# A two-layer mixer with mixture of experts: a semaphore for each piece of expert weights, down weights released in halves, and expert sums in another order

## The chip, the cores and the metric

One core of a Trainium2 chip runs the whole program. Its engines work side by side and are tied together by semaphores: TensorE (PE) for products and transposes, VectorE (DVE), ScalarE (ACT), GpSimd (POOL), and SyncE (SP), which here does nothing but issue DMAs. Weights come from HBM by DMA. The metric is the device time of one execution in microseconds (us), the median over runs.

## What is computed

Two layers work on 256 latent and 256 context tokens of width 1024. Each has three token mixers, merged by gates, and then a mixture of 32 experts, of which each token takes two. Layer 0 sends all 512 tokens through its experts, layer 1 only the 256 latent ones. All is fp32. What the change touches is the second half of a layer:

```
def hierarchical_moe(h, ...):          # top-1 group, top-2 expert
    ...
    return expert_dispatch(h, experts, weights, w_gate, w_up, w_down)
def run_block(args):                   # one expert
    xb, e = args
    return (jax.nn.silu(xb @ w_gate[e]) * (xb @ w_up[e])) @ w_down[e]
...
x = x + mx[5] * fx                     # fx: weighted sum of a token's two experts
...
y = xf * lax.rsqrt(jnp.mean(xf * xf, axis=-1, keepdims=True) + NORM_EPS)   # next norm
```

## The kernel before

**Experts.** A layer's expert loop runs over 32 experts in pairs (`expert`, `s` is the expert's place in its pair). An expert has 64 slots of tokens; where the router sends it more (`n > BLK`), `more_slots` works through an extra block of 32 ahead of the 64. PE does, for each expert: `gate_up`, the product of its tokens with gate and up weights (line L795, 16 matmuls, which the profile shows as 32 records); then half of the preparation of the next pair (picking its token rows by a one-hot product, L779, or turning them, L787); `turn_h`; and `down`, the down product (L808, 8 matmuls, 16 records). ACT and DVE do the activation between the two and copy the result out, and ACT writes it to the HBM table `y_rows`.

**Weights.** An expert has four pieces of gate/up weights and two of down weights, 1 MB each, each two rows of the contraction: `gate_up` uses piece k // 2 in its step k. SP issues all pieces on one queue. Gate/up weights have two slots in the loop (a third, with id 2, serves only expert 1), down weights two. All four pieces of a slot raise one semaphore (`gu_in`), and PE waits for the sum of four ahead of `gate_up`; so with the two down pieces (`wd_in`). A slot is given back in pieces on the gate/up side (`gu_used` rises after each second step of `gate_up`, and `next_gate_up` on SP waits piece by piece), and as a whole on the down side (`down_done`, `next_down`). SP works through its list in order: four gate/up pieces of an expert, then its two down pieces, each with its wait.

**Sums and the next norm.** After the loop, POOL gathers the two expert rows of each token from `y_rows`, in tiles of 128 tokens: four tiles in layer 0, two in layer 1. Per tile, ACT scales the first row (L1239), DVE adds the second one, scaled (L1658), PE turns the sum (L919), DVE adds it to the stream (`add_tile`, L1652), ACT squares it (`square_tile`, L1232), and PE averages the squares over the width (`mean_tile`, L909) into PSUM bank 6 for all tiles. Then one root on ACT (L980), one reciprocal on DVE (L1315) and the norm's scaling (L1331; at the very end L1327) follow. ACT's order at the end of layer 0 is: scale 0, scale 1, square 0, scale 2, square 1, scale 3, square 2, two weight tiles of the next layer (`round_first`), square 3, root. DVE does its part of those weight tiles and the next layer's gains after the last addition.

Of the kernel before, what the change touches and what calls it, by code (L numbers as in the profile page):

```python
# [24 lines left out]
ACT = mybir.ActivationFunctionType  # L25
# [112 lines left out]
def hybrid_block(nc, t, out, counts=None):  # L138
# [4 lines left out]
    with ctx:  # L143
# [40 lines left out]
        eps = sb("eps", [P, 1])  # L184
        route_w = sb("route_w", [P, 2, 4])
# [6 lines left out]
        def part(base, kib, size, *dims, dt=F32):  # L192
# [68 lines left out]
        names = """ident_in mean_in consts_in rows_in_done vecs_in router_in swa_in wst0 wst1 wst2 wst3 wst4 wst5 mwt0 mwt1 mwt2 mwt3 mwt4 mwt5 cond_in bias0 bias1 bias2  # L261
            bias3 gu_in0 gu_in1 gu_in2 wd_in0 wd_in1 y_saved yo_saved yt_saved yg_got0 yg_got1 yg_got2 yg_got3 out_saved
# [7 lines left out]
            gu_used silu_done hid_done hidt_done hidt_copied down_done y_copied  # L270
# [6 lines left out]
        gu_in, wd_in = [g[f"gu_in{i}"] for i in range(3)], [g[f"wd_in{i}"] for i in range(2)]  # L277
# [103 lines left out]
        def _(sp):  # L381
# [35 lines left out]
            def load_gate_up(e_src, slot, pieces=range(4)):  # L417

                for i in pieces:
                    sp.dma_start(wgu[slot][i], e_src(t["w_exp_gate_up"])[:, 2 * i:2 * i + 2]).then_inc(gu_in[slot].sem, 16)  # L420

            def load_down(e_src, slot):

                for i in range(2):
                    sp.dma_start(wd[slot][i], e_src(t["w_exp_down"])[:, 2 * i:2 * i + 2]).then_inc(wd_in[slot].sem, 16)
# [21 lines left out]
            for l in range(DEPTH):  # L447
# [19 lines left out]
                def next_down(e, s):  # L467
                    sp.wait_ge(g["down_done"].sem, NE * l + e - 1)
                    load_down(lambda w: w[l, bass.ds(e, 1)].rearrange("a p k n -> (a p) k n"), s)
# [16 lines left out]
        def _(pe):  # L486
# [115 lines left out]
            for l in range(DEPTH):  # L602
# [202 lines left out]
                def down(bank, src, w, sem):  # L805
                    for k in range(4):
                        for j in range(2):
# [6 lines left out]
                def more_slots(more, slot, landed, s, two):  # L814
# [15 lines left out]
                    pe.wait_ge(gu_in[slot].sem, landed * 64)  # L830
                    for k in range(KC):
                        at = MORE * k
# [8 lines left out]
                    pe.wait_ge(wd_in[s].sem, (PAIRS * l + two + 1) * 32)  # L841
                    for k in range(4):
                        for j in range(4):
# [15 lines left out]
                def expert(e, two, s, slot, nth):  # L859
# [20 lines left out]
                    pe.wait_ge(gu_in[slot].sem, landed * 64)  # L880
                    gate_up(s, wgu[slot])
# [11 lines left out]
                    pe.wait_ge(wd_in[s].sem, (PAIRS * l + two + 1) * 32)  # L893
                    down(4, hid_t, wd[s], g["down_done"].sem)
# [9 lines left out]
                def mean_tile(tile):  # L904
                    if tile == 0:
                        claim(6)
                    pe.wait_ge(g["sq_done"].sem, g["sq_done"].at(*after, tile))
                    for c in range(KC):
                        mm = pe.matmul(pv_bank[:, tile * P:(tile + 1) * P], mean_w[:, :], sq_tile[tile % 2][:, c, :],  # L909
                                       start=(c == 0), stop=(c == KC - 1))  # L910
                    mm.then_inc(g["mean_done"].sem, g["mean_done"].tick(*after, tile))

                for tile in range(nt):
# [14 lines left out]
                free[6] = (g["rstd_sqrt"], after)  # L928
# [10 lines left out]
        def _(act):  # L939
# [22 lines left out]
            def squares(l, which):  # L962
                w = width(l) if which != "n1" else NTOK
                if which == "n1" and l == 0:
                    act.wait_ge(g["in_copied"].sem, g["in_copied"].at(KC - 2))
                    act.wait_ge(g["prep"].sem, g["prep"].at("xt", KC - 1))
                for c in range(KC):
# [7 lines left out]
                root(l, which, KC - 1)  # L975

            def root(l, which, last):
                w = width(l) if which != "n1" else NTOK
# [868 lines left out]
```

## Time and profile before

| | |
|---|---|
| runs | 2032.97, 2038.33, 2045.43 us; median 2038.33 |
| profiled execution | 2040.66 us (span on the page 2041.3), mean granted PE clock 0.954 |
| busy | PE 1796.3 us (88%), DVE 694.2 (34%), ACT 519.4 (25%), POOL 154.9 (8%) |
| expert loop of layer 0 | first product 625.8, end of last down product 1121.2 |
| expert loop of layer 1 | first product 1507.1, end of last down product 2003.3 |
| bytes moved | 550.71 MB, mean 270 GB/s over the span |

A row of a timeline gives start, duration, engine, source line, operation, output and input, and in brackets how long the engine was idle ahead of it and what ended that. "DMA" as the releaser is the landing of a transfer.
### The profile page before, as it was taken

The page shows a single profiled execution, that of the slowest core. Times are in us where ns is not written, and L with a number is a line of the kernel's source. Part 1 is how long each engine was busy: PE and PEld are TensorE (multiplying, and loading weights), DVE is VectorE, ACT ScalarE, POOL GpSimd, SP SyncE. Part 2 cuts the span into 40 slices and gives each one's busy share as a digit, 9 for nine tenths or more (in the row PEclk, how much of TensorE's full clock was granted, in tenths as well). Part 3 has the DMA queues.
Part 4 walks back from the last instruction along what each step waited for, and adds up shares of the span by engine and source line. Part 5 has one row for each costly group of instructions (what it writes and reads, how often), then busy time and mean ns, then how long its engine had stood idle before and what let it go on. Part 6 is the DMA issues. An engine that isn't in the chain of part 4 may idle for free.

```text
span 2041.3 us, 26468 instructions
## 1 busy us (share of the span) xinstructions
PE 1796.3 (88%) x9291; PEld 1022.3 (50%) x9292; DVE 694.2 (34%) x1451; ACT 519.4 (25%) x1053; POOL 154.9 (8%) x190
## 2 busy tenths in 40 slices
PE   6999899999968999899999599999858998988985
PEld 3756666678743343334433487779723333333323
DVE  4465255445452111111111665663531111111113
ACT  4344444432230011011110454551311111011011
POOL 0062031000000000000000224310000000000000
PEclk9999999999988999999999699999979999999997
DMA  8356565223266999998999243334496999999992
GB/s 311 129 184 212 202 220 185 102 69 102 73 262 240 379 422 421 421 397 349 420 421 400 91 136 90 113 94 141 157 399 231 409 403 421 421 421 421 420 421 83
DMA packets 96058, 550.71 MB, mean 270 GB/s; under 512 B 14162, under 2 KB 15650, under 8 KB 42724
## 3 DMA queue, kind: packets, MB, share of 16 engines
q1 hardware_dynamic: 83108, 526.89, 65.8%
q0 software_dynamic: 4224, 11.35, 1.9%
q10 hardware_dynamic: 8640, 11.28, 1.5%
q8 instruction: 59, 0.97, 0.2%
q14 instruction: 27, 0.22, 0.0%
HBM read 537.15 MB, written 12.32 MB: 269 GB/s over the span
## 4 chain that ended last, share of the span: by engine, by line
PE 64%; DMA 20%; DVE 7%; ACT 4%; issue 3%; SPq 0%; ACTq 0%; POOL 0%; POOLq 0%; DVEq 0%
DMA moe<-in_w_exp_gate_up_dram 18%; PE ps L795 17%; PE ps L507 8%; PE ps L509 8%; PE ps L508 8%; PE ps L808 6%; PE ps L779 3%; PE ps L729 2%; PE ps L656 2%; PE ps L685 2%; PE ps L667 2%; DMA moe<-in_w_mod_dram 1%; PE ps L835 1%; DVE w_lo L1297 1%; PE ps L565 1%
## 5 line engine op out<-in xcount | busy, mean ns | idle before, releaser
L795 PE MATMUL ps<-moe,ht 128*64 128x512 f32 x1984 | 466.8, 626 | 69.4 <-DMA moe<-in_w_exp_gate_up_dram 47.8
L795 PEld LDWEIGHTS ps<-moe,ht 128*64 128x64 f32 x1984 | 145.7, 144 | 383.3 <-issue 309.4
L1633 DVE TENSOR_TENSOR arena<-aux,ps 128x256 f32<-128x256 f32 x64 | 27.0, 422 | 702.7 <-ACT aux L1205 702.7
L507 PE MATMUL ps<-ht_hi,w_hi 128*128 128x512 f32 (+1 forms) x704 | 253.3, 360 | 3.0 <-ACT arena L1092 1.6
L509 PE MATMUL ps<-ht_hi,w_lo 128*128 128x512 f32 (+1 forms) x704 | 244.7, 348 | 0.0
L508 PE MATMUL ps<-ht_lo,w_hi 128*128 128x512 f32 (+1 forms) x704 | 244.5, 347 | 0.0
L808 PE MATMUL ps<-moe,arena 128*64 128x512 f32 x1024 | 233.8, 598 | 2.6
L1297 DVE TENSOR_TENSOR w_lo<-ws,w_hi 128x1024 fp32r<-128x1024 f32 (+1 forms) x122 | 150.2, 1235 | 223.3 <-ACT w_hi L997 223.3
L997 ACT ACTIVATE w_hi<-ws 128x1024 fp32r<-128x1024 f32 (+1 forms) x122 | 125.2, 1026 | 183.7 <-PE ps L509 146.7
L507 PEld LDWEIGHTS ps<-ht_hi,w_hi 128*128 128x128 f32 x704 | 134.2, 191 | 25.5 <-issue 9.7
L509 PEld LDWEIGHTS ps<-ht_hi,w_lo 128*128 128x128 f32 x704 | 134.2, 191 | 16.9
L508 PEld LDWEIGHTS ps<-ht_lo,w_hi 128*128 128x128 f32 x704 | 134.5, 191 | 15.3
L808 PEld LDWEIGHTS ps<-moe,arena 128*64 128x64 f32 x1024 | 67.8, 136 | 131.4 <-issue 120.9
L1209 ACT ACTIVATE arena<-ps 128x512 f32<-128x512 f32 x64 | 38.2, 597 | 373.4 <-PE ps L808 373.4
L1750 POOL DMA_INDIRECT arena<-y_rows,dest x8 | 7.8, 979 | 1480.5 <-ACTq L1224 1478.6
L1205 ACT ACTIVATE aux<-ps 128x256 f32<-128x256 f32 x64 | 24.6, 385 | 357.0 <-PE ps L795 357.0
L779 PE MATMUL ps<-hr_hi,pick 128*128 128x512 f32 x204 | 88.8, 435 | 9.4 <-DVE pick L1559 9.4
L779 PE MATMUL ps<-hr_lo,pick 128*128 128x512 f32 x204 | 82.4, 404 | 0.0
L1205 ACT ACT_TABLE_LOAD x32 | 41.1, 1283 | 138.0 <-issue 138.0
L779 PEld LDWEIGHTS ps<-hr_hi,pick 128*128 128x128 f32 x204 | 39.6, 194 | 42.0 <-issue 30.8
L1733 POOL DMA_DIRECT2D aux<-in_rpb_a_dram x64 | 39.7, 628 | 180.0 <-DVE stat L1408 127.5
L667 PEld LDWEIGHTS ps<-ident,moe 128*128 128x128 f32 x320 | 34.3, 141 | 33.6 <-issue 31.9
(253 smaller groups left out, 2186.6 us busy)
## 6 DMA issues: line engine op xcount, KB each, us to landing
moe<-in_w_exp_gate_up_dram SPq DMA_DIRECT2D x248, 1024.0 KB, 19.9
moe<-in_w_exp_down_dram SPq DMA_DIRECT2D x128, 1024.0 KB, 17.9
ws<-in_w_in_dram SPq DMA_DIRECT2D x92, 512.0 KB, 4.3
moe<-in_w_mod_dram SPq DMA_DIRECT2D x29, 1536.0 KB, 6.7
y_rows<-arena ACTq DMA_DIRECT2D x164, 64.0 KB, 5.6
ws<-in_w_branch_dram SPq DMA_DIRECT2D x16, 512.0 KB, 3.6
ws<-in_w_out_dram SPq DMA_DIRECT2D x16, 512.0 KB, 3.5
ws<-in_w_exp_gate_up_dram SPq DMA_DIRECT2D x6, 1024.0 KB, 19.0
```

Of the source, the lines that this page charges most:

```text
L507: pe.matmul(ps[:, bank, 0:cols], w[:, k, :], a_hi, start=(i == 0), stop=False)
L508: pe.matmul(ps[:, bank, 0:cols], w[:, k, :], a_lo, start=False, stop=False)
L509: mm = pe.matmul(ps[:, bank, 0:cols], w_lo[:, slot, k, :], a_hi, start=False, stop=(k == rows[-1]))
L656: mm = pe.matmul(score_bank[:, hh, 0:n], q_of(kind)[HD * hh:HD * hh + HD, pair, q0:q0 + P], kt_of(kind, 2 * pair + hh)[:, keys], start=Tru ...
L667: mm = pe.transpose(prob_bank[:, tile, hh * P:(hh + 1) * P], prob[h % 2][:, hh, tile * P:(tile + 1) * P], ident[:, :])
L685: mm = pe.matmul(pv_bank[HD * hh:HD * hh + HD, 0:SEQ], v_of(kind, 2 * pair + hh, tile + (4 - n)), prob_t[hh][:, tile, :], start=(tile == 0 ...
L779: mm = pe.matmul(ps[:, 7 * half, :], pick[:, tile, :], rows[:, tile, 512 * half:512 * half + 512], start=(tile == 0 and rows is hr_hi), st ...
L795: mm = pe.matmul(ps[BLK * j:BLK * j + BLK, 2, :].rearrange("p (g n) -> p g n", g=2), xg[:, k, BLK * s:BLK * s + BLK], w[k // 2][:, k % 2, ...
L808: mm = pe.matmul(ps[BLK * j:BLK * j + BLK, bank, :], src[:, k % 2, BLK * (k // 2):BLK * (k // 2) + BLK], w[k // 2][:, k % 2, 512 * j:512 * ...
L997: nc.scalar.activation(high_part(i)[:, 0:m], ws[:, slot, 0:m, :], ACT.Copy) \
L1205: nc.scalar.activation(act_g, ps[:, 2, 0:256], ACT.Silu).then_inc(g["silu_done"].sem, 1)
L1297: v.tensor_tensor(w_lo[:, ws_slots[item], 0:m], ws[:, ws_slots[item], 0:m, :], high_part(i)[:, 0:m].bitcast(F32), ALU.subtract).then_inc(g ...
```

## The change

Each piece has a semaphore of its own (`gu_in` 3 x 4, `wd_in` 2 x 2), and PE waits for a piece right ahead of the step that uses it first, in `gate_up`, `down` and `more_slots`. The down product raises `down_used` after each of its two halves, and SP loads the halves of a down slot one by one. At the end of a layer ACT takes the order scale, scale, scale, square; averages alternate between banks 6 and 7; root and reciprocal are done for each tile; the next layer's first weight tiles and gains go ahead of the sums; and an activation with a one-column result (`load_roots`) loads ACT's table for roots ahead of the sums and ahead of the second norm.

```
-                sp.dma_start(wgu[slot][i], ...).then_inc(gu_in[slot].sem, 16)
+                sp.dma_start(wgu[slot][i], ...).then_inc(gu_in[slot][i].sem, 16)
...
                 def next_down(e, s):
-                    sp.wait_ge(g["down_done"].sem, NE * l + e - 1)
-                    load_down(lambda w: ..., s)
+                    for i in range(2):
+                        sp.wait_ge(g["down_used"].sem, 2 * (NE * l + e - 2) + i + 1)
+                        load_down(lambda w: ..., s, (i,))
...
-                def gate_up(s, w):
+                def gate_up(s, slot, landed):
+                    w = wgu[slot]
                     for k in range(KC):
+                        if k % 2 == 0:
+                            pe.wait_ge(gu_in[slot][k // 2].sem, landed * 16)
...
-                    mm.then_inc(sem, 1)
+                            if k % 2 and j:
+                                mm.then_inc(g["down_used"].sem, 1)
...
-                    pe.wait_ge(gu_in[slot].sem, landed * 64)
-                    gate_up(s, wgu[slot])
+                    gate_up(s, slot, landed)
...
                 def mean_tile(tile):
-                    if tile == 0:
-                        claim(6)
+                    claim(6 + tile % 2)
...
-                    if tile:
-                        mean_tile(tile - 1)
+                    if tile >= 2:
+                        mean_tile(tile - 2)
                 for bank in (2, 3, 4, 5):
                     claim(bank)
-                mean_tile(nt - 1)
+                for tile in range(nt - 2, nt):
+                    mean_tile(tile)
...
+            def load_roots():
+                nc.scalar.activation(root_one[:, :], eps[:, :], ACT.Sqrt)
...
+                load_roots()
+                if l + 1 < DEPTH:
+                    round_first(l + 1)
                 for tile in range(nt):
                     nc.scalar.activation(hr[:, tile, :], yg[tile][0], ACT.Copy, ...)
-                    if tile:
-                        square_tile(tile - 1)
-                if l + 1 < DEPTH:
-                    round_first(l + 1)
-                square_tile(nt - 1)
-                root(*after, nt - 1)
+                    if tile >= 2:
+                        square_tile(tile - 2)
+                for tile in range(nt - 2, nt):
+                    square_tile(tile)
+                    if nt > 2:
+                        root_tile(tile - 2)
+                for tile in range(nt - 2, nt):
+                    root_tile(tile)
```

The first place is PE's gate/up product of the first expert of a pair, in the loop over pairs. `moe_51` holds the weights, `ht_49` the tokens, `gu_in1` is the semaphore of slot 1. Before:

```order
L864 UNCONDITIONAL_BRANCH
L880 REGISTER_ALU
L795 MATMUL ps<-moe_51,ht_49 64x512 [waits gu_in1]
L795 MATMUL ps<-moe_51,ht_49 64x512 x15
L883 REGISTER_ALU
```

The same place afterwards (`gu_in10` to `gu_in13` are the four pieces of slot 1):

```order
L876 UNCONDITIONAL_BRANCH
L799 REGISTER_ALU
L801 MATMUL ps<-moe_51,ht_49 64x512 [waits gu_in10]
L801 MATMUL ps<-moe_51,ht_49 64x512 x3
L801 MATMUL ps<-moe_51,ht_49 64x512 [waits gu_in11]
L801 MATMUL ps<-moe_51,ht_49 64x512 x3
L801 MATMUL ps<-moe_51,ht_49 64x512 [waits gu_in12]
L801 MATMUL ps<-moe_51,ht_49 64x512 x3
L801 MATMUL ps<-moe_51,ht_49 64x512 [waits gu_in13]
L801 MATMUL ps<-moe_51,ht_49 64x512 x3
```

The single wait ahead of 16 matmuls is now four, one ahead of each four; no other instruction was added between them.

The second place is ACT at the end of layer 0. `route_w` marks the scalings, `arena<-xt` the squares, `aux<-ps,eps` the roots. Before:

```order
L1239 ACTIVATE arena<-arena,route_w 128x1024 [waits yg_got1]
L1232 ACTIVATE arena<-xt 128x1024 [waits comb_added]
L1239 ACTIVATE arena<-moe,route_w 128x1024 [waits yg_got2]
L1232 ACTIVATE arena<-xt 128x1024 [waits comb_added]
L1239 ACTIVATE arena<-moe,route_w 128x1024 [waits yg_got3]
L1232 ACTIVATE arena<-xt 128x1024 [waits mean_done,comb_added]
L997 ACTIVATE w_first<-ws 128x1024 [waits out_done,wst5]
L997 ACTIVATE w_hi<-ws 128x1024 [waits out_done,wst0]
L1232 ACTIVATE arena<-xt 128x1024 [waits mean_done,comb_added]
L980 ACT_TABLE_LOAD
L980 ACTIVATE aux<-ps,eps 128x512 [waits mean_done]
```

Afterwards:

```order
L1013 ACTIVATE w_first<-ws 128x1024 [waits out_done,wst5]
L1013 ACTIVATE w_hi<-ws 128x1024 [waits out_done,wst0]
L1261 ACTIVATE arena<-arena,route_w 128x1024 [waits yg_got0,dest_set]
L1261 ACTIVATE arena<-arena,route_w 128x1024 [waits yg_got1]
L1261 ACTIVATE arena<-moe,route_w 128x1024 [waits yg_got2]
L1251 ACTIVATE arena<-xt 128x1024 [waits comb_added]
L1261 ACTIVATE arena<-moe,route_w 128x1024 [waits yg_got3]
L1251 ACTIVATE arena<-xt 128x1024 [waits comb_added]
L1251 ACTIVATE arena<-xt 128x1024 [waits mean_done,comb_added]
L992 ACTIVATE aux<-ps,eps 128x128 [waits mean_done]
L1251 ACTIVATE arena<-xt 128x1024 [waits mean_done,comb_added]
L992 ACTIVATE aux<-ps,eps 128x128 [waits mean_done] x3
```

The third scaling went ahead of the first square and the fourth ahead of the second, the two weight tiles ahead of all scalings, and one root of 512 columns became four of 128.

The third place is PE at the end of layer 1, with two tiles. `hr` lies in `arena`; `mean_w` marks the averages. Before:

```order
L919 MATMUL ps<-ident,arena 128x128 [waits comb]
L919 MATMUL ps<-ident,arena 128x128 x7
L909 MATMUL ps<-arena,mean_w 128x128 [waits sq_done]
L909 MATMUL ps<-arena,mean_w 128x128 x7
L909 MATMUL ps<-arena,mean_w 128x128 [waits comb_added,sq_done]
```

Afterwards:

```order
L929 MATMUL ps<-ident,arena 128x128 [waits comb]
L929 MATMUL ps<-ident,arena 128x128 x7
L918 MATMUL ps<-arena,mean_w 128x128 [waits comb_added,sq_done]
L918 MATMUL ps<-arena,mean_w 128x128 x7
L918 MATMUL ps<-arena,mean_w 128x128 [waits sq_done]
```

The wait for the second tile's addition (`comb_added`) moved from the second average to the first.

## Rows read from the trace of the kernel before

**Rows 1.** The page, chain of work that ended last: shares of the span by line.

```profile
DMA moe<-in_w_exp_gate_up_dram 18%; PE ps L795 17%; PE ps L507 8%; PE ps L509 8%; PE ps L508 8%; PE ps L808 6%; PE ps L779 3%; PE ps L729 2%; PE ps L656 2%; PE ps L685 2%; PE ps L667 2%; DMA moe<-in_w_mod_dram 1%; PE ps L835 1%; DVE w_lo L1297 1%; PE ps L565 1%
```

**Rows 2.** Stretches: start:end, length, busy time by engine, PE clock, DMA share, GB/s.

```profile
692.00:752.00 60.00, 59.13 (x278) 23.62 (x274) 9.74 (x18) 7.80 (x12) 0.00 (x0) 1.00 1.01 410
896.00:972.00 76.00, 71.91 (x423) 30.17 (x417) 12.22 (x24) 8.82 (x14) 0.00 (x0) 0.98 0.90 356
972.00:1113.00 141.00, 134.25 (x620) 54.18 (x618) 24.34 (x45) 16.23 (x25) 0.00 (x0) 0.99 1.01 421
1637.00:1655.00 18.00, 17.57 (x85) 6.36 (x82) 2.47 (x5) 2.31 (x4) 0.00 (x0) 1.00 0.99 367
1836.37:1851.64 15.27, 12.20 (x60) 4.32 (x60) 2.47 (x5) 1.01 (x3) 0.00 (x0) 1.00 1.01 421
```

**Rows 3.** Timeline of PE, 1840 to 1910: two gate/up products of layer 1.

```profile
1851.63 8.78 PE L795 MATMUL ps<-moe,ht 128*64 128x512 f32 x32 [2.63 <-DMA moe<-in_w_exp_gate_up_dram]
...
1866.90 7.09 PE L795 MATMUL ps<-moe,ht 128*64 128x512 f32 x32 [0.59 <-DMA moe<-in_w_exp_gate_up_dram]
```

**Rows 4.** Timeline of SP's DMA issues, 840 to 1110: weights of expert 22.

```profile
954.28 5.48 SPq L420 DMA_DIRECT2D moe<-in_w_exp_gate_up_dram  x4
967.13 0.85 SPq L425 DMA_DIRECT2D moe<-in_w_exp_down_dram  x2
```

**Rows 5.** Timeline of PE, 836 to 960: expert 16 and expert 17's extra block.

```profile
865.68 8.78 PE L795 MATMUL ps<-moe,ht 128*64 128x512 f32 x32 [2.94 <-DMA moe<-in_w_exp_gate_up_dram]
...
888.68 5.35 PE L835 MATMUL ps<-moe,arena 128*32 128x256 f32 x64 [0.60 <-DVE arena L1617]
```

**Rows 6.** Timeline of PE, 1060 to 1125: experts 28, 30 and 31 of layer 0.

```profile
1062.75 8.78 PE L795 MATMUL ps<-moe,ht 128*64 128x512 f32 x32 [2.45 <-DMA moe<-in_w_exp_gate_up_dram]
...
1093.28 7.09 PE L795 MATMUL ps<-moe,ht 128*64 128x512 f32 x32 [1.64 <-DMA moe<-in_w_exp_gate_up_dram]
...
1108.56 7.09 PE L795 MATMUL ps<-moe,ht 128*64 128x512 f32 x32 [0.50 <-DMA moe<-in_w_exp_gate_up_dram]
...
1117.54 3.65 PE L808 MATMUL ps<-moe,arena 128*64 128x512 f32 x16
```

**Rows 7.** Timeline of PE, 1983 to 2005: last expert of layer 1.

```profile
1989.04 8.70 PE L795 MATMUL ps<-moe,ht 128*64 128x512 f32 x32 [2.29 <-DMA moe<-in_w_exp_gate_up_dram]
```

**Rows 8.** Timeline of PE's weight loads, 1100 to 1106: start of a down product.

```profile
1104.40 0.20 PEld L808 LDWEIGHTS ps<-moe,arena 128*64 128x64 f32 x4 [0.35 <-issue]
1104.89 0.14 PEld L808 LDWEIGHTS ps<-moe,arena 128*64 128x64 f32 x2 [0.28 <-issue]
```

**Rows 9.** Timeline of DVE, 1126 to 1166: sums, additions, next norm.

```profile
1137.72 2.15 DVE L1652 SCALAR_TENSOR_TENSOR xt<-ps,modv,xt 128x128 f32<-128x128 f32 x8
1142.04 1.28 DVE L1658 SCALAR_TENSOR_TENSOR arena<-moe,route_w,arena 128x1024 f32<-128x1024 f32 x1 [2.16 <-ACT arena L1239]
...
1148.76 4.22 DVE L1652 SCALAR_TENSOR_TENSOR xt<-ps,modv,xt 128x128 f32<-128x128 f32 x16
...
1161.67 2.46 DVE L1331 SCALAR_TENSOR_TENSOR ht<-xt,gain,aux 128x256 f32<-128x256 f32 x6
```

**Rows 10.** Timeline of ACT, 1126 to 1166: first scaling, a weight tile, table load, root.

```profile
1132.12 1.15 ACT L1239 ACTIVATE arena<-arena,route_w 128x1024 f32<-128x1024 f32 x1 [10.22 <-DMA arena<-y_rows,dest]
...
1151.91 1.04 ACT L997 ACTIVATE w_first<-ws 128x1024 fp32r<-128x1024 f32 x1
...
1154.86 1.28 ACT L980 ACT_TABLE_LOAD   x1
1157.56 0.69 ACT L980 ACTIVATE aux<-ps,eps 128x512 f32<-128x512 f32 x1 [1.42 <-PE ps L909]
```

**Rows 11.** Timeline of all engines, 1983 to 2042: averages and reciprocal at the end.

```profile
2022.64 5.64 PE L909 MATMUL ps<-arena,mean_w 128*128 128x128 f32 x32 [1.19 <-ACT arena L1232]
...
2028.90 1.75 DVE L1315 RECIPROCAL aux<-aux 128x256 f32<-128x256 f32 x1 [5.25 <-ACT aux L980]
```

**Rows 12.** The page, DMA issues: queue, KB each, median us from issue to landing.

```profile
moe<-in_w_exp_gate_up_dram SPq DMA_DIRECT2D x248, 1024.0 KB, 19.9
```

More of the change, by code:

```diff
@@ L419, in load_gate_up, with load_down @@
                 for i in pieces:
[L420 to L425, printed above, removed]
+                    sp.dma_start(wgu[slot][i], e_src(t["w_exp_gate_up"])[:, 2 * i:2 * i + 2]).then_inc(gu_in[slot][i].sem, 16)
+            def load_down(e_src, slot, pieces=range(2)):
+                for i in pieces:
+                    sp.dma_start(wd[slot][i], e_src(t["w_exp_down"])[:, 2 * i:2 * i + 2]).then_inc(wd_in[slot][i].sem, 16)
             held = []
@@ L803, in turn_h, with down @@
                     mm.then_inc(g["hidt_done"].sem, 1)
-                def down(bank, src, w, sem):
+                def down(bank, src, s, landed):
+                    w = wd[s]
                     for k in range(4):
+                        if k % 2 == 0:
+                            pe.wait_ge(wd_in[s][k // 2].sem, landed * 16)
                         for j in range(2):
@@ L892, in expert @@
                     pe.wait_ge(g["y_copied"].sem, done + 1)
[L893 to L894 removed]
+                    down(4, hid_t, s, PAIRS * l + two + 1)
                 for e in range(2 * AHEAD_PAIRS):
@@ L974, in squares, with root @@
                         .then_inc(g["sq_done"].sem, g["sq_done"].tick(l, which, c))
[L975 to L978 removed]
+                root(l, which, KC - 1, slice(0, w))
+            def root(l, which, last, cols, *tile):
                 act.wait_ge(g["mean_done"].sem, g["mean_done"].at(l, which, last))
[L980 to L981 removed]
+                bank = 6 + tile[0] % 2 if tile else 6
+                nc.scalar.activation(rs[:, cols], ps[:, bank, cols], ACT.Sqrt, bias=eps[:, 0:1]) \
+                    .then_inc(g["rstd_sqrt"].sem, g["rstd_sqrt"].tick(l, which, *tile))
+            def load_roots():
+                nc.scalar.activation(root_one[:, :], eps[:, :], ACT.Sqrt)
             def round_weights(l, job, ahead=2):
@@ L1226, in _, with root_tile @@
                 after = (l + 1, "n1") if l + 1 < DEPTH else (l, "fin")
+                def root_tile(tile):
+                    root(*after, tile, slice(tile * P, (tile + 1) * P), tile)
                 def square_tile(tile):
@@ L1316, in reciprocal_rms, with reciprocal_tile @@
                 dve.wait_ge(g["rstd_done"].sem, g["rstd_done"].at(l, which))
+            def reciprocal_tile(l, which, tile):
+                cols = slice(tile * P, (tile + 1) * P)
+                dve.wait_ge(g["rstd_sqrt"].sem, g["rstd_sqrt"].at(l, which, tile))
+                v.reciprocal(rs[:, cols], rs[:, cols]).then_inc(g["rstd_done"].sem, g["rstd_done"].tick(l, which, tile))
+                if tile == (4 if which == "n1" else 2) - 1:
+                    dve.wait_ge(g["rstd_done"].sem, g["rstd_done"].at(l, which, tile))
             def leave_h(l, c):
@@ L1350, in _ @@
                 w_all = width(l)
-                gains(l, 0)
-                if l:
-                    gains(l, 1)
-                    leave_first(l)
-                    reciprocal_rms(l, "n1")
+                if l == 0:
+                    gains(l, 0)
+                else:
+                    for tile in range(4):
+                        reciprocal_tile(l, "n1", tile)
                 scale_norm(l, "n1")
@@ L1663, in _ @@
                 dve.wait_ge(g["comb_added"].sem, g["comb_added"].at(l, nt - 1))
-            reciprocal_rms(DEPTH - 1, "fin")
+            for tile in range(2):
+                reciprocal_tile(DEPTH - 1, "fin", tile)
             scale_norm(DEPTH - 1, "fin")
```

32 lines of the change are left out of this document (20 added, 12 removed).

## The prediction

> **What bounds the kernel now.** I read the chain of work that ended last first [rows 1]: most of it is TensorE (PE), but its largest single entry is no instruction. It is the landing of gate/up weights, 18% of the span, some 367 us. Since that share is an average over two expert loops, I went on with the view of stretches [rows 2]. Its GB/s column reads 421 wherever DMA is never idle: from 972 to 1113 (end of the first loop) and in a single expert of the second one (15.27 us, of which PE is busy 12.20 at a granted clock of 1.00, its full level of 2.4 GHz). There DMA sets the pace, and no order of waits moves it: 6.29 MB of weights an expert at 421 GB/s is 14.9 us, the rest is rows of y. So the change can pay only where DMA was idle (692 to 752: 410; 896 to 972: 356; 1637 to 1655: 367), and after the last piece has landed, when PE alone is late.
>
> What PE does in a bound expert is in [rows 3]: 2.63 us without work, then 32 matmul records in 8.78; in the next one 0.59, then 7.09. The longer idle time costs 1.69 more, because the product begins at the lower clock. In both cases all four pieces had to be there, while at 421 GB/s a piece (1.05 MB) takes 2.49 us and its quarter of the product 7.09/4 = 1.77. PE could have been through three quarters when the fourth landed.
>
> **The change part by part.** *Products piece by piece.* Three places count.
>
> (a) Expert 16 of layer 0, just ahead of one whose extra block of 32 slots keeps PE longer. Its product starts at 865.68 after 2.94 idle and takes 8.78 [rows 5]. Afterwards one quarter is left when the last piece lands: 8.78 - 1.77 = 7.0 earlier. From there to about 1060 PE hardly waits, so the whole chain moves by 7.0. Expert 17's extra product (888.68 now) would start at 881.7; its last gate/up piece lands, two down pieces and four of its own behind the one at 865.65, at 865.65 + 6 x 2.49 = 880.6. That margin of 1.1 us is thin.
>
> (b) Then PE runs on until DMA stops it. Before, it waited 2.45, 1.64 and 0.50 in experts 28, 30 and 31 and lost 1.69 to the clock: 6.3 [rows 6]. If DMA moves ahead with PE, these go. DMA does: its issues at 954.28 and 967.13 wait for PE's releases [rows 4] and come 7.0 earlier, the second another half down product earlier (3.65/2 = 1.8). So DMA gets back 8.8 of the 11.7 it loses between 896 and 972 (76 x (1 - 356/421)). Two ends compete. PE's: 1121.2 (1117.54 + 3.65) less 7.0, 6.3 and the 1.5 of the next paragraph. DMA's: the last piece at 1108.5 - 8.8 - 1.5 = 1098.2, then 1.77, the 1.9 from product to down product, and 3.65: 1105.5. PE's is 1106.4, later, and decides.
>
> (c) The last expert of layer 1: its product, 8.70 after 2.29 idle [rows 7], becomes one quarter: 6.9. The down pieces land 2.5 and 5 us behind the last gate/up piece; the down product's halves want them 3.7 and 5.5 behind it. They are there.
>
> *Down weights released in two.* The first half is free 1.8 earlier. That matters once per stretch, where DMA runs dry on exactly this release: in layer 0, 60 x (1 - 410/421) = 1.6 us is lost between 692 and 752, of which I take 1.5 (ends 0 and 1.8); in layer 1, 18 x (1 - 367/421) = 2.3, part of it paced by PE's gate/up releases, which don't move: 1.0 (ends 0 and 2.3).
>
> *More waits.* Each product has four semaphores to look at instead of one, each down product two. PE's rows get no longer by it, the waits ride on matmuls. Weight loads that ran ahead may stop at them. The nearest row is the first load of a down product, which waits for several semaphores that are already up: 0.35 idle against 0.28 between loads [rows 8], so 0.07. On PE's path in layer 0 stand 15 experts x 4 waits: between 0 and 4.2; since the loads overlap running matmuls I take 1.0.
>
> So layer 0's loop: 7.0 + 6.3 + 1.5 - 1.0 = 13.8 (low end 6.8, which is the last product's 7.09 - 1.77 = 5.3 and 1.5; high end 16). Layer 1's: 6.9 + 1.0 = 7.9 (5.3 to 9.2).
>
> A rule speaks against waiting in small bits. First the rows: 0.59 idle left the clock up, 2.63 brought half of it for 8 of 32 records [rows 3]. The Trainium skill (TensorE: Matmul & The Clock Gate, section "A second HAM failure mode: psum-queue depth-cycling") says that frequent short idles between groups of matmuls make the clock swing between its levels even where no single one is long. In bound experts the change makes such idles, 2.49 - 1.77 = 0.7 after each piece. By the rows the sum stays as it is; by the rule it is the third rival's. No row here shows idles of 0.7 in a series.
>
> *Expert sums, end of layer 0.* Before, ACT scales tile 2 only after squaring tile 0, and tile 3 after squaring tile 1, so sums (1.28) and additions (2.15) on DVE have pauses between them: the first addition ends at 1139.87, the last at 1152.98 [rows 9], 13.1 for 2 sums and 3 additions, which are 9.0 of work. Afterwards the sums don't wait for squares, and this work can run back to back: 4.1 earlier, last addition at 1148.9. It wants tile 3 on DVE at 1143.3, so gathered by about 1142. From the last addition to the norm's first product it was 8.7 (to 1161.67), with a root of 0.69 for 512 columns in it [rows 10]. Afterwards both last averages follow the last addition, since they stand behind the claim of all transpose banks: 5.64 for two [rows 11]; then a root of 128 columns, at most 0.69, I take 0.4, and a reciprocal of 128, 0.95, a little over half of the 1.75 for 256 [rows 11]; with 0.3 of hops 7.3, so 1.4 less. That is 5.5, and the clock may be up for the averages: I take 6.0 (3.3 if gathers or a low clock hold the middle, 7.5 if neither). The gains and the first two weight tiles, moved ahead, lie in the 10.22 in which ACT waits for the first gather [rows 10], at no cost; without that cover ACT's half of them alone would be 2 x 1.04. The table of roots, 1.28, moves there too; where it was, it ran beside the averages and cost nothing.
>
> *Second norm.* The same table load leaves the place between last square and root, where the last average runs beside it: between 0 and 1.28 in each layer, I take 0.3, in sum 0.6. Its new place is ahead of ACT's wait for the first output product.
>
> *End of layer 1.* Only two tiles, so no round is saved. The first average now waits for the second tile's addition: 1.0 later than 2022.64. The reciprocal per tile gives back 0.8 (1.75 to 0.95), the root perhaps 0.1 [rows 11]. Sum -0.1 (-1.0 to 1.0).
>
> **Sum.** 13.8 + 7.9 + 6.0 + 0.6 - 0.1 = 28.2. Against the profiled execution's 2040.66 that is 2012.5. The median of the runs shown lies 2.3 lower, which would give 2010.1; I predict **2010**. The runs of this kernel spread from 2032.97 to 2045.43, so a change under 1% (20 us) can hardly be told from none.
>
> **The rivals.** *The gap of layer 0 stays.* Expert 17's pieces are late, or the issues stay bunched: PE's 7.0 is eaten at the thin margin of (a), DMA comes no earlier, and the loop gains its low end, 6.8. Sum 21.2, time 2017. For it: 1.1 us of margin. Against: the releases come from PE, which is earlier by itself. Chance 0.13.
>
> *It doesn't do what it says.* The four pieces are in flight together and share the 16 DMA engines; landing takes 19.9 us from issue [rows 12], in which several pieces could advance side by side and land together. Then PE still waits for the last one with all its work to do; (a), (b) and (c) go, and 1.5 + 1.0 + 6.5 = 9 remains: 2029. For it: nothing shows single landings. Against: they are issued 1.8 apart on one queue, the 19.9 fits eight pieces in line at 2.49. Chance 0.08.
>
> *The clock swings at the short waits.* Last quarter, the way to the down product and the down product (1.77 + 1.9 + 3.65 = 7.3) then run at half speed, 7.3 more, which takes (a) and (c) and most of (b): 28.2 - 7.0 - 6.9 - 5 = 9, about 2029. Against: 0.59 idle did no harm. Chance 0.06.
>
> *Slower than before.* Where PE stays at the lower clock through the DMA-bound stretches, an expert's 12.20 becomes 24.4, 9.1 more than DMA's 15.27. Eighteen experts of layer 1 are bound so; from four in a row on (28.2/9.1 = 3.1) the gain is gone, with six it is 2067 - some 26 above before. For it: the rule above. Against: a PE that is late has no idle time, and in the row of 8.78 the clock was back within one product. Chance 0.04.
>
> **How the numbers follow.** The forecast has 0.69, between 2002 (16 + 9.2 + 7.5 + 1.9 + 1.0 = 35.6 off, 3 below by the runs' spread) and 2018. To hold 8 in 10, the range must reach over the first rival and its spread: 2002 to 2023. Faster by over 1% means under 2018: most of the forecast and half the first rival, 0.73; slower 0.04; the rest 0.23.
>
> **What would show it.** Waits of products for weights become many short ones of under 1 us each, and the last product of a loop has pauses within it. Stretch rows of the first loop: 356 becomes 400 or more. Wrong by: products that still wait 2 to 3 us and then run through (second rival), PE clock below 0.9 in bound experts of both parities (third), a first-loop end less than 10 us earlier with the pauses there (first).

## The result

The changed kernel takes 2014.61 us, median of four runs (2012.05 to 2019.42), against 2038.51 before (2032.97 to 2045.43). The ratio is 0.9885, 95% interval 0.9868 to 0.9901: 1.15% or 23.4 us faster, where 28.2 were forecast against the profiled execution and 2010 as the time. A second set of runs gave 0.9869 (0.9853 to 0.9886). Below, a loss against the changed kernel in us is the difference to the mean of these two ratios, 0.9877, times 2039; the intervals leave some 4 to 5 us of doubt in each.

The two profiled executions lie 28.6 apart (2040.66 and 2012.05), their spans 31.0. That is 7 more than the medians (23.9), so the table below holds some 7 us of the spread between executions, and a term of it that matches the forecast within a few us says little by itself. In the seven profiles of this study that have both expert loops as changed, word for word, layer 0's loop takes 480.4 to 482.2 and layer 1's 482.3 to 488.4. By places, from the timelines of the two:

| from, to | before | after | change | forecast |
|---|---|---|---|---|
| start to first product of layer 0's expert loop | 625.8 | 624.3 | -1.5 | -0.3 |
| layer 0's loop, to the end of its last down product | 495.4 | 480.4 | -15.0 | -13.8 |
| to the first scaling of the next norm | 40.5 | 35.8 | -4.7 | -6.0 |
| to the first product of layer 1's loop | 345.4 | 344.5 | -0.9 | -0.3 |
| layer 1's loop | 496.2 | 486.0 | -10.2 | -7.9 |
| to the output's DMA | 33.6 | 34.8 | +1.2 | +0.1 |

(The last column takes the terms of the prediction, the 0.6 of the second norm halved between the layers.)

**The profile after.** The page's chain of work that ended last; in [rows 1] the weights' landing had 18%:

```profile
PE ps L801 15%; DMA moe<-in_w_exp_gate_up_dram 12%; PE ps L817 8%; PE ps L510 8%; PE ps L512 8%; PE ps L511 8%; PE ps L782 4%; SPq L422 2%; PE ps L732 2%; PE ps L659 2%; PE ps L688 2%; PE ps L670 2%; PE ps L568 1%; DVE w_lo L1321 1%; SPq L427 1%
```

The stretches of the changed kernel that answer to [rows 2] (start:end, length, busy time by engine, PE clock, DMA share, GB/s):

```profile
692.00:752.00 60.00, 59.13 (x276) 25.26 (x272) 10.57 (x20) 7.99 (x12) 0.00 (x0) 1.00 1.02 421
...
896.00:972.00 76.00, 71.89 (x403) 29.74 (x401) 13.76 (x27) 9.03 (x14) 0.00 (x0) 0.98 0.98 397
972.00:1113.00 141.00, 129.63 (x606) 52.78 (x602) 24.80 (x50) 18.65 (x29) 1.33 (x2) 0.99 0.99 408
...
1700.00:1960.00 260.00, 225.35 (x998) 74.36 (x992) 38.92 (x76) 28.22 (x43) 0.00 (x0) 1.00 1.01 421
```

410 became 421 and 356 became 397; the 408 of the third row comes from the loop, whose weights now end within it. The last row is the bound part of layer 1: DMA is as saturated as before, so its pace is unchanged, 15.28 an expert (16 of them from 1711.43 to 1955.94, by the starts of their products), and the PE clock there is 1.00.

The timeline of PE, changed kernel: the expert ahead of the extra block in layer 0 ([rows 5]), the last expert of layer 0 ([rows 6]) and the last one of layer 1 ([rows 7]):

```profile
854.09 1.94 PE L801 MATMUL ps<-moe,ht 128*64 128x512 f32 x8 [0.41 <-DMA moe<-in_w_exp_gate_up_dram]
856.58 1.94 PE L801 MATMUL ps<-moe,ht 128*64 128x512 f32 x8 [0.55 <-DMA moe<-in_w_exp_gate_up_dram]
859.28 1.94 PE L801 MATMUL ps<-moe,ht 128*64 128x512 f32 x8 [0.76 <-DMA moe<-in_w_exp_gate_up_dram]
862.22 1.94 PE L801 MATMUL ps<-moe,ht 128*64 128x512 f32 x8 [1.01 <-DMA moe<-in_w_exp_gate_up_dram]
...
878.27 5.16 PE L846 MATMUL ps<-moe,arena 128*32 128x256 f32 x64 [0.52 <-DVE arena L1648]
...
1090.98 5.32 PE L801 MATMUL ps<-moe,ht 128*64 128x512 f32 x24
1097.18 1.94 PE L801 MATMUL ps<-moe,ht 128*64 128x512 f32 x8 [0.88 <-DMA moe<-in_w_exp_gate_up_dram]
1101.02 3.65 PE L817 MATMUL ps<-moe,arena 128*64 128x512 f32 x16
...
1958.26 1.94 PE L801 MATMUL ps<-moe,ht 128*64 128x512 f32 x8 [0.44 <-DMA moe<-in_w_exp_gate_up_dram]
1960.75 1.94 PE L801 MATMUL ps<-moe,ht 128*64 128x512 f32 x8 [0.55 <-DMA moe<-in_w_exp_gate_up_dram]
1963.54 1.94 PE L801 MATMUL ps<-moe,ht 128*64 128x512 f32 x8 [0.85 <-DMA moe<-in_w_exp_gate_up_dram]
```

One wait of up to 2.9 us ahead of 32 records has become waits of 0.4 to 1.0 ahead of eight, four of them in the first product shown and three in the last. PE doesn't wait less: from 1690 to the end of layer 1 PE's waits for gate/up weights sum to 33.6 us in 20 waits before and 32.6 in 51 after, the longest 2.6 and 0.9. Where DMA sets the pace, a wait that is cut in pieces is still a wait. What pays is what PE has left when the last piece lands: 1.94 instead of 8.7.

### The profile page after: what moved, and what is told of

It reads as the page before. It is cut to its first block, busy times and chain, and to the rows that moved or that the text cites. A ratio compares the mean times of both kernels' runs of the same rounds, so it can differ in the third digit from the quotient of the medians.

```text
span 2010.3 us, 26521 instructions
## 1 busy us (share of the span) xinstructions
PE 1779.2 (89%) x9291; PEld 1010.1 (50%) x9292; DVE 693.2 (34%) x1455; ACT 520.9 (26%) x1061; POOL 155.6 (8%) x190
## 4 chain that ended last, share of the span: by engine, by line
PE 67%; DMA 13%; DVE 8%; ACT 4%; SPq 4%; issue 4%; POOL 0%; ACTq 0%; POOLq 0%; DVEq 0%
PE ps L801 15%; DMA moe<-in_w_exp_gate_up_dram 12%; PE ps L817 8%; PE ps L510 8%; PE ps L512 8%; PE ps L511 8%; PE ps L782 4%; SPq L422 2%; PE ps L732 2%; PE ps L659 2%; PE ps L688 2%; PE ps L670 2%; PE ps L568 1%; DVE w_lo L1321 1%; SPq L427 1%
## 5 line engine op out<-in xcount | busy, mean ns | idle before, releaser
L801 PE MATMUL ps<-moe,ht 128*64 128x512 f32 x1984 | 456.3, 603 | 59.7 <-DMA moe<-in_w_exp_gate_up_dram 39.4
L801 PEld LDWEIGHTS ps<-moe,ht 128*64 128x64 f32 x1984 | 136.5, 138 | 369.4 <-issue 259.6
## 6 DMA issues: line engine op xcount, KB each, us to landing
moe<-in_w_exp_gate_up_dram SPq DMA_DIRECT2D x248, 1024.0 KB, 20.3
```

What stands on the lines that cost most here:

```text
L801: mm = pe.matmul(ps[BLK * j:BLK * j + BLK, 2, :].rearrange("p (g n) -> p g n", g=2), xg[:, k, BLK * s:BLK * s + BLK], w[k // 2][:, k % 2, ...
```

## The experiments

**All four pieces awaited, the rest as changed.**

```
 for k in range(KC):
-    if k % 2 == 0:
-        pe.wait_ge(gu_in[slot][k // 2].sem, landed * 16)
+# ahead of the loop, in gate_up and more_slots:
+for i in range(4):
+    pe.wait_ge(gu_in[slot][i].sem, landed * 16)
```

> The changed kernel, but each gate/up product waits for all four of its pieces before its first step; down weights released in halves and the sums as changed. Theory (the piecewise wait carries most of the gain): expert 16's product and those of experts 28, 30 and 31 of layer 0 wait 2 to 3 us again and run through in 7.1 to 8.8, the loop of layer 0 ends 12 to 14 us later, the last product of layer 1 takes its whole 8.7 behind the last piece, 6.8 later; 2014.6 + 19 to 21 = 2034 to 2036. Rival (the four pieces land nearly together, the gain is from the halves and the sums): under 3 us later, 2015 to 2018.

Measured: 2032.74, ratio 0.9971 (0.9954 to 0.9988), 19 us above the changed kernel. The theory holds, the second rival of the prediction (pieces that land together) falls. The timeline of PE (experts 16 and 30 of layer 0, 29 and 31 of layer 1):

```profile
862.54 7.09 PE L801 MATMUL ps<-moe,ht 128*64 128x512 f32 x32 [2.95 <-DMA moe<-in_w_exp_gate_up_dram]
...
1087.70 7.09 PE L801 MATMUL ps<-moe,ht 128*64 128x512 f32 x32 [2.65 <-DMA moe<-in_w_exp_gate_up_dram]
...
1945.18 8.78 PE L801 MATMUL ps<-moe,ht 128*64 128x512 f32 x32 [2.27 <-DMA moe<-in_w_exp_gate_up_dram]
...
1975.71 7.09 PE L801 MATMUL ps<-moe,ht 128*64 128x512 f32 x32 [2.30 <-DMA moe<-in_w_exp_gate_up_dram]
```

Layer 0's loop is 491.2 long, 10.8 more than in the changed kernel and less than the 12 to 14 expected: the product of expert 16 ran in 7.09 after 2.95 idle, where before the change it took 8.78 after 2.94 [rows 5]. Of experts 28, 30 and 31 only 30 waited over 2 us; 28 and 31 waited 1.54 and 0.82. The clock's 1.69 thus isn't owed to the wait alone. The last two rows say the same: 2.27 and 2.30 idle, 8.78 and 7.09. The kernel before had shown it too: beside the rows of [rows 3] it has, in layer 1's expert 30, 7.09 after 2.62:

```profile
1973.77 7.09 PE L795 MATMUL ps<-moe,ht 128*64 128x512 f32 x32 [2.62 <-DMA moe<-in_w_exp_gate_up_dram]
```

Two stretches of the run that awaits all four, the first one in layer 0 and the second in layer 1 (the changed kernel has 397 GB/s and a clock of 1.00 there):

```profile
896.00:972.00 76.00, 71.27 (x403) 30.62 (x401) 14.06 (x28) 8.82 (x14) 0.00 (x0) 0.98 0.91 369
...
1700.00:1960.00 260.00, 227.14 (x986) 88.34 (x986) 39.27 (x77) 26.81 (x42) 0.00 (x0) 0.95 1.01 421
```

**Piecewise in layer 0 only.** In layer 1 all four are awaited, by the same edit under `if l`.

> The changed kernel, but only layer 0 waits piece by piece; in layer 1 each product waits for all four. Theory: layer 0's loop as in the changed kernel (480 from its first product to the end of the last down product); in layer 1 the last piece lands as early as in the changed kernel (478.6 after the loop's first product), since DMA sets the pace, and only the last product is late by 6.8; 2021.4. Rival (the piecewise waits also give pieces back earlier, and that brought DMA's 3.4 us in layer 1): the last piece lands at 481 to 482, 2023 to 2025.

Measured: 2024.23, ratio 0.9928 (0.9905 to 0.9950), 10.4 above the changed kernel, 9 below the one that waits for all four. Both layers have their share. The last product of layer 1, in the timeline of PE:

```profile
1965.74 7.09 PE L803 MATMUL ps<-moe,ht 128*64 128x512 f32 x32 [0.72 <-DMA moe<-in_w_exp_gate_up_dram]
```

It begins 480.5 after the loop's first product, between the 478.6 of the theory and the rival's 481. This can't be read closer: in the seven profiles that have both loops as changed, the last quarter begins 474.9 to 480.9 after it.

**Down halves released together.**

```
 for i in range(2):
-    sp.wait_ge(g["down_used"].sem, 2 * (NE * l + e - 2) + i + 1)
+    sp.wait_ge(g["down_used"].sem, 2 * (NE * l + e - 2) + 2)
```

> The changed kernel, but both halves of a down slot are loaded only when the whole down product is over. Theory (the early half feeds DMA where it runs dry): GB/s below 421 in the first 130 us of both loops, the last piece of layer 1 lands 3.4 later after the loop's first product (482 instead of 478.6), layer 0 ends 1 to 2 later; 2014.6 + 4.4 to 5.4 = 2019 to 2020. Rival (layer 0 is paced by PE from expert 18 on and has room, and DMA's 3.4 in layer 1 come from PE's earlier gate/up releases): under 1 us, 2014 to 2016.

Measured: 2023.25, ratio 0.9918 (0.9899 to 0.9937), 8.4 above the changed kernel: more than the theory asked. The stretches of layer 0:

```profile
621.00:692.00 71.00, 59.24 (x256) 23.02 (x258) 13.72 (x36) 6.49 (x10) 0.00 (x0) 0.93 0.73 275
692.00:752.00 60.00, 59.14 (x277) 23.95 (x274) 9.90 (x19) 8.16 (x12) 0.00 (x0) 1.00 1.01 416
...
896.00:972.00 76.00, 71.46 (x403) 30.02 (x401) 14.94 (x29) 8.83 (x14) 0.00 (x0) 0.98 0.95 386
```

DMA loses in three stretches, not in one: the changed kernel has 421 and 397 in the second and third (above; 421 to 422 and 395 to 403 in the seven profiles), and in the first 66.5 us from the loop's first product it has 303 GB/s (299 to 305), this run 293. Layer 0's loop is 4.3 longer than the changed kernel's and 2.5 longer than the longest of the seven. Expert 3's product took 8.8 instead of 7.1 here, by the clock; but it took 8.5 to 8.8 in three of the seven as well, whose loops are only 0.7 to 0.9 longer than the changed kernel's, so most of the 4.3 isn't the clock's.

**The halves alone, on the kernel before.** The down product raises its semaphore after each half and SP loads half by half; nothing else.

> The kernel before with one part of the change alone: the down product raises its semaphore after each half, and SP loads the halves of a down slot one by one. Theory, from the runs so far (the early half pays in every stretch in which DMA runs dry, three in layer 0 and two in layer 1): first loop 4.1 shorter (491.3 from its first product), second one 3.3 to 3.5 shorter; 2038.5 - 7.5 = 2031. Rival, the sum of the prediction (it pays once in each layer, 1.5 and 1.0): 2036.

Measured: 2036.22, ratio 0.9984 (0.9970 to 0.9998), 3.3 us below before. The interval leaves 0.4 to 6.1, so the theory of 7.5 falls; the rival, my own sum of 2.5, lies within it. In the profile the two loops are 0.6 and 1.3 shorter than before. In the stretches:

```profile
692.00:752.00 60.00, 59.13 (x276) 24.03 (x273) 10.16 (x19) 8.16 (x12) 0.00 (x0) 1.00 1.01 418
...
896.00:972.00 76.00, 71.90 (x401) 29.89 (x399) 12.22 (x24) 8.82 (x14) 0.00 (x0) 0.98 0.91 358
```

The third stretch keeps its hole (356 before, 358): its issues follow PE, and PE is as late there as before. The halves give 3.3 (0.4 to 6.1) without piecewise waits and 8.4 (some 4 to 13) with them. These intervals overlap, so the medians don't show that the parts depend on each other. The profiles speak for it: layer 0's loop gains 0.6 without the piecewise waits and 2.5 or more with them. That PE's earlier steps let the half release act between 896 and 972 fits the 358 and 397. At the loop's start it can't be the piecewise gate/up waits: the run that awaits all four has 299 GB/s over the first 66.5 us, this one 294. The two differ there in the down product, which waits piece by piece only in the former; no run undoes that wait alone, so this part stays open.

**The expert loops alone, end of a layer as before.** All of the change in the loops; scalings, squares, averages, roots, reciprocals, gains and first weight tiles in the old order.

> The changed expert loops (a semaphore for each piece, down weights in halves) with the end of a layer and the roots as before the change. In the changed kernel POOL's first gather begins 5.8 us after ACT issued the last expert's rows, before 3.2. Theory (those rows now share the DMA engines with the next layer's first weight tiles, since the loop ends nearer to the landing of the last expert piece): the gather stays 5.8 behind, from the end of layer 0's last down product to the norm's first scaling it is 43 us, and layer 1's end is 1.4 shorter than in the changed kernel; 2014.6 + 7.3 - 1.4 = 2020 to 2021. Rival (ACT's new order holds the gather back): 3.2 again, 40.5 us; 2014.6 + 4.7 - 1.4 = 2018.

Measured: 2021.75, ratio 0.9908 (0.9891 to 0.9926), 6.3 above the changed kernel, where the prediction gave this part 6.5 (6.0 + 0.6 - 0.1). From the end of the loop to the norm it is 42.5. The timeline of ACT's DMA issue and POOL's gather, the sixth column being the line:

```profile
1106.44 0.80 ACTq L1167 DMA_DIRECT2D y_rows<-arena  x2
1112.25 1.06 POOL L1767 DMA_INDIRECT arena<-y_rows,dest  x1 [800.91 <-ACTq L1234]
```

The gather is 5.8 behind the last rows with ACT's old order too; here the theory holds and the rival falls. Its other part missed: layer 1's end was to be 1.4 shorter than in the changed kernel and is 0.1 shorter, because the averages took 6.45 with the old order too. Awaiting all four pieces with ACT's new order gives 3.2, because that loop ends 11 us later, when the weight tiles are through.

**The changed kernel again.**

> The changed kernel once more, on the chip of the next three: 2014 to 2017, gather 5.8 behind the rows, 35.8 from the end of layer 0's loop to the norm's first scaling. Theory on the end of layer 1: the averages begin 20.5 after the loop's end whenever the first one waits for the second addition, and take 5.6 to 6.7, by when the clock rises.

Measured: 2013.88, ratio 0.9869. The gather is 6.0 behind the rows, the end of layer 0 36.1, layer 0's loop 480.4; the averages begin 20.3 after layer 1's loop and take 6.2.

**Weight tiles held back until the gathers are through.** In SP's list, ahead of layer 1's third weight tile:

```
+if l and i == 2:
+    sp.wait_ge(g["comb_half"].sem, g["comb_half"].at(l - 1, 3))
```

> The changed kernel, but SP issues only two of the next layer's first six weight tiles behind the last expert piece; the other four, 2 MB, wait until the fourth tile of expert rows has been gathered and scaled. Theory (those tiles hold up the last expert's rows): rows to first gather 3.2 instead of 5.8, the whole end of layer 0 33.2 instead of 35.8, and the four tiles are still there before PE wants them; 2.6 less than the changed kernel, 2012. Rival (the rows are held up by something else, or PE then waits for the tiles): gather still at 5.8, or the first products of the next layer wait; 2014.6 or more.

Measured: 2014.25, ratio 0.9862 (0.9845 to 0.9880): no difference that the medians can tell from the changed kernel's 0.9869 on the same chip; the 2.6 expected are within the doubt. Locally the theory holds: the gather is 3.2 behind the rows and the end of layer 0 is 33.7 long. But from the norm to layer 1's first product it is 348.0, against 344.5 and 343.7 in the two profiles of the changed kernel. (The profiled execution took 2021.04, the longest of the four; its start and its loops are longer too, so the rows below account for the 3.5 of this place alone.) Here is where PE lost it, in the timeline of DVE, POOL and PE:

```profile
1320.95 2.81 DVE L1457 TENSOR_SCALAR moe<-moe,stat 128x512 f32<-128x512 f32 x2
...
1322.22 1.26 POOL L1780 TENSOR_TENSOR aux<-aux,colok 128x512 f32<-128x512 f32 x1 [0.18 <-DMA aux<-in_rpb_a_dram]
...
1323.91 1.07 PE L672 MATMUL ps<-ident,moe 128*128 128x128 f32 x8 [2.76 <-DVE moe L1457]
1326.12 0.55 PE L512 MATMUL ps<-ht_hi,w_hi 128*128 128x256 f32 x1 [1.15 <-DVE w_lo L1323]
```

Two DVE steps that take 1.76 together in the changed kernel take 2.81 where POOL's second pair of operations begins beside them; PE waits 2.76 for them (1.69 in the changed kernel) and 1.15 for the next one, and the matmuls behind that take 0.41 instead of 0.28 for a while. The run with both edits has the like (2.84 and 2.56) and 349.1; no other profile of this study has more than 345.6. Whether the held tiles bring DVE and POOL together here, or chance does, stays open.

**The first average ahead of the claim, at the end of layer 1.**

```
+lag = 2 if nt > 2 else 1
-if tile >= 2:
-    mean_tile(tile - 2)
+if tile >= lag:
+    mean_tile(tile - lag)
 ...
-for tile in range(nt - 2, nt):
+for tile in range(nt - lag, nt):
     mean_tile(tile)
```

> The changed kernel, but at the end of layer 1 the first average stands ahead of the claim of the transpose banks, as before the change; roots and reciprocals stay one for each tile. Theory (the first average waits needlessly for the second addition): averages begin 1.2 earlier, 19.4 after the loop's end, and the norm's scaling about as much earlier, 27.3 instead of 28.6; 1.2 less, 2013.4. Rival (the clock decides: PE works at its lower level until it has run for a while, so an earlier start with a pause behind it gains nothing): 28.4 to 28.6, no difference.

Measured: 2014.56, ratio 0.9871 (0.9855 to 0.9888), no difference that the medians can tell. In the trace the averages begin 1.2 earlier (19.4 after the loop's end) and the norm comes 27.35 after it, against 28.6 and 28.0 in the two profiles of the changed kernel: the theory's size, in one profile. The 1.2 is too small for the medians.

**Both edits.**

> The changed kernel with both of these edits: the four weight tiles held until the gathers are through, and layer 1's first average ahead of the claim. Theory: the two gains add, 2.6 + 1.2 = 3.8, 2010.8. Rival (either gives nothing): 2012 to 2014.6.

Measured: 2013.45, ratio 0.9864 (0.9846 to 0.9882). The median lies in the rival's range, but the theory's 3.8 is within the doubt. No version here is faster than the change beyond what the runs can tell.

**Both edits, tiles held only until the rows are saved.** SP waits for `prep`, which ACT raises when the last rows are in `y_rows`.

> The changed kernel with layer 1's first average ahead of the claim, and four of the next layer's first six weight tiles held only until the last expert's rows are saved, not until they are gathered. Theory: rows to first gather 3.2 again; the 2 MB now run beside the gathers, which puts the first scaling 0 to 3 later behind the gather (6.8 in the changed kernel); 1.5 to 4 less in all than the changed kernel's 2014, 2010 to 2012.5. Rival (the tiles cost the gathers as much as they cost the rows): 2013 to 2014.

Measured: 2015.29, ratio 0.9884 (0.9867 to 0.9901). The timeline of issues, gather and first scaling:

```profile
1107.28 0.80 ACTq L1176 DMA_DIRECT2D y_rows<-arena  x2
1109.62 1.97 SPq L436 DMA_DIRECT2D ws<-in_w_in_dram  x4
...
1110.46 1.06 POOL L1789 DMA_INDIRECT arena<-y_rows,dest  x1 [798.33 <-ACTq L1243]
...
1121.15 1.15 ACT L1264 ACTIVATE arena<-arena,route_w 128x1024 f32<-128x1024 f32 x1 [8.09 <-DMA arena<-y_rows,dest]
```

Rows to gather 3.2 again, but gather to scaling 10.7 instead of 6.8: the 2 MB now hold up the gathers. The rival's mechanism holds, its time (2013 to 2014) is within the doubt. In these runs the tiles cost their time wherever rows move beside them.

## Why the prediction was right, and where its sizes were off

**Expert 16 and the thin margin.** Counted from the loop's first product, its gate/up product ends 8.75 earlier (248.65 to 239.90); 7.0 from the pieces and 1.5 from the halves were forecast. Expert 17's extra product, forecast for 881.7, starts at 878.27 and waits for DVE, not for weights. The first rival (the gap stays) fell at this row: 397 GB/s, where it would have kept 356; with all four pieces awaited it is 369.

**The two competing ends.** From 886.73 on PE waits for no weights until the very last piece, for 0.88; the ends of PE and DMA lie within 1 us of each other, as forecast (1106.4 and 1105.5), and the loop ends at 1104.67. Undoing the waits alone took back 10.8 of the 13.3 given to the pieces in this loop. The clock's 1.69, counted in (a) and again within (b), makes 3.4 and covers the difference: when the waits were put back, experts 16 and 30 waited 2.95 and 2.65 and still took 7.09. Here a size was off, in the other direction than the halves.

**The last expert of layer 1.** 6.9 forecast; the product behind the last piece shrank from 8.70 to 1.94, 6.8, and the down pieces were there. The profile with the wait undone in layer 1 alone is 7.1 longer in this loop, its median 10.4 (some 5 of doubt).

**The halves** were the mis-sized term: 2.5 forecast, 3.3 (0.4 to 6.1) alone, 8.4 in company. I took them to matter once per stretch and gave them one stretch of layer 0; in the changed kernel they act at the loop's start and between 896 and 972 too.

**The sum.** The pieces were forecast at 7.0 + 6.3 + 6.9 - 1.0 = 19.2, and undoing their waits lost 19. That agreement is partly luck: in the profile the loops lose 10.8 and 12.2, where 12.3 and 6.9 were forecast, and other places give some back, 1.8 of it at the end of layer 0 (34.0 instead of 35.8), where the rows no longer meet the weight tiles. The sums lost 6.3, with 6.5 forecast. Undone one by one, pieces, halves and sums lose 34 (some 8 of doubt) where the whole change gained 25 by the same ratios, so the parts overlap. The forecast time of 2010 lies 4.6 below the median; which place that comes from can't be read, since the profiled pair gained more than forecast.

**The extra waits** cost nothing: products without a wait take 7.04 and 7.09 as before. The 1.0 taken for them was too much.

**The end of layer 0.** Rows of the changed kernel that answer to [rows 9, 10], in the timeline of all engines:

```profile
1105.56 0.80 ACTq L1173 DMA_DIRECT2D y_rows<-arena  x2
...
1111.36 1.06 POOL L1786 DMA_INDIRECT arena<-y_rows,dest  x1 [800.03 <-ACTq L1240]
...
1118.19 1.15 ACT L1261 ACTIVATE arena<-arena,route_w 128x1024 f32<-128x1024 f32 x1 [4.24 <-DMA arena<-y_rows,dest]
...
1130.34 4.43 DVE L1683 SCALAR_TENSOR_TENSOR xt<-ps,modv,xt 128x128 f32<-128x128 f32 x16
...
1135.23 3.81 PE L918 MATMUL ps<-arena,mean_w 128*128 128x128 f32 x32 [0.87 <-DVE xt L1683]
...
1139.48 0.95 DVE L1345 RECIPROCAL aux<-aux 128x128 f32<-128x128 f32 x1 [0.83 <-ACT aux L992]
1140.46 2.46 DVE L1362 SCALAR_TENSOR_TENSOR ht<-xt,gain,aux 128x256 f32<-128x256 f32 x6
```

From the first scaling to the end of the last addition it is 16.6 instead of 20.9, 4.3 less (4.1 forecast). From there to the norm 5.7 instead of 8.7: 3.0 less where 1.4 was forecast and 0.5 allowed for the clock. The two last averages take 3.81, not 5.64: they begin when the last square is nearly done and run at a granted clock of 1.00, where before 1152 to 1158 had 0.63 and 0.78. The term forgotten is ahead of both: the last rows reach `y_rows` later. Before, the six weight tiles for layer 1, which SP issues behind the last expert piece, were through (the last one at 1121.45) when the last rows were sent (1122.16). The change brought the loop's end close behind the last piece: the last four tiles landed between 1105.93 and 1109.90, and the rows, sent at 1105.56, behind them at 1110.27. ACT's wait for them is in its timeline:

```profile
1110.56 1.28 ACT L997 ACT_TABLE_LOAD   x1 [5.25 <-DMA y_rows<-arena]
```

Rows to gather 5.8 instead of 3.2: 2.6 of the gain came back at once. Holding four tiles back brought the 3.2 again, in three runs.

**End of layer 1.** The first average waits for the second addition, begins 1.2 later after the loop's end (1.0 forecast), and roots and reciprocals for each tile give 1.0 back (0.9). The 1.0 beyond is the averages themselves:

```profile
1991.55 6.65 PE L918 MATMUL ps<-arena,mean_w 128*128 128x128 f32 x32 [2.46 <-DVE xt L1683]
...
1999.62 3.26 DVE L1358 SCALAR_TENSOR_TENSOR ht<-xt,colv,aux 128x256 f32<-128x256 f32 x8
```

6.65 against 5.64 [rows 11]; in the old order they took 6.45 in one profile and 4.18 in another, so the 1.0 is no more than the spread between executions. The granted clock goes with it: 1.00 throughout the 4.18, and 0.50 from 1991 to 1997 in the 6.65. The row of the 4.18, from the run with the halves alone:

```profile
2016.37 4.18 PE L911 MATMUL ps<-arena,mean_w 128*128 128x128 f32 x32 [1.33 <-ACT arena L1234]
```

**The clock at short waits** (third and fourth rival). In the bound part of layer 1 the granted clock was 1.00 over 260 us with pauses of 0.4 to 0.9 ahead of three of each product's four quarters, and 0.95 in the same stretch of the run that waits for all four. The Trainium skill (TensorE: Matmul & The Clock Gate, section "A second HAM failure mode: psum-queue depth-cycling") warned of such pauses; this trace does not agree: beside the short pauses the clock stayed at 1.00, and the run with waits of 2.3 in every second expert had the 0.95. One reading of the prediction was wrong in a detail: the product of 8.78 in [rows 3] does not begin at the lower clock. Its first two records take 0.64, as those of the product of 7.09 do; then the granted clock is 0.50 (1852.7 to 1855.2, records of 1.06), and from 1855.9 on it is 1.00 (records of 0.59).

**The second norm.** 0.6 forecast for both layers. The start of layer 0's loop lies between 624.3 and 628.2 in the changed kernel and its variants, so the 1.5 of the table above can't be told from chance, nor the 0.9 of layer 1. In place the term can be read: from the start of ACT's last square to that of the root it is 1.94 in layer 0 and 1.73 in layer 1 in the three profiles with the old place of the table load, 1.84 to 1.85 and 1.21 in the nine with the new one. That is 0.1 and 0.5, together the 0.6 forecast. (The upper end of the range took 1.9 for this term, where its own bounds add up to 2.6; nothing hangs on it.)

## What to carry to other kernels

In a stretch that DMA saturated, finer waits hardly changed the sum of the waits (33.6 and 32.6): look for what is left to do when the last byte lands, and for the places where the compute engine becomes the late one, and count only those. When the end of a loop moves closer to the last landing, look at what the queue sends next, since the loop's own results now share the engines with it. Gains of parts that feed one another need not be a sum: measure each alone and undone. And a table of places from two executions also holds their spread: look at how one unchanged place varies before matching terms.

## What the hardware showed that I had not expected

- The same idle time ahead of a product brought the lower clock or not: 2.94 and 8.78 before, 2.95 and 7.09 in the run that waits for all four; 2.27 and 2.30 in one run with 8.78 and 7.09; 2.63 and 2.62 in the kernel before with 8.78 and 7.09.
- Two DVE steps that take 1.76 with the first of them beside a POOL operation took 2.81 with both beside one, and PE, having waited for them, ran at a granted clock of 0.50 from 1326 to 1329. A step takes 0.47 where POOL is idle, and the two took 1.37 and 1.52 here, each ending 0.28 after the POOL operation that began 0.18 and 0.02 before it. The Trainium skill (SBUF — State Buffer, section "Who interferes with whom") says that such steps of the two engines block each other for a whole instruction; the trace agrees: each step ended only after the POOL operation of 1.27 or 1.26 that had begun before it.
- The last expert's rows, 128 KB, arrived 2.6 us later while the last four of six weight tiles, 2 MB, were landing, and with 2 MB moving beside the gathers the first scaling came 3.9 later behind the first gather.
